# Expert rows of the sparse tokens begin when half of tile 1's heads are picked, in a two-block transformer kernel on one core

## What is computed

```python
def peer_ffn(h, w_q, sub_k1, sub_k2, expert_u, expert_v):
    q = (ht @ w_q).reshape(T, PEER_HEADS, PEER_QDIM)
    s1 = jnp.einsum('thd,nd->thn', q[..., :PEER_HALF], sub_k1).astype(jnp.float32)
    s2 = jnp.einsum('thd,nd->thn', q[..., PEER_HALF:], sub_k2).astype(jnp.float32)
    v1, i1 = lax.top_k(s1, PEER_TOPK)
    v2, i2 = lax.top_k(s2, PEER_TOPK)
    cand = (v1[..., :, None] + v2[..., None, :]).reshape(T, PEER_HEADS, PEER_TOPK * PEER_TOPK)
    ...
    vals, pos = lax.top_k(cand, PEER_TOPK)
    experts = jnp.take_along_axis(cand_idx, pos, axis=-1)
    gates = jax.nn.softmax(vals, axis=-1)
    ...
        u = expert_u[ec]
        a = jnp.einsum('cd,chkd->chk', xc, u).astype(jnp.float32)
        w = (jax.nn.gelu(a) * gc).astype(xc.dtype)
        return jnp.einsum('chk,chkd->cd', w, expert_v[ec])
```

## Time and profile before

| | |
|---|---|
| median of 3 runs | 1836.27 us (1835.15 to 1836.65) |
| the profiled execution: its time | 1835.7 us |
| its span, first to last instruction | 1833.9 us |
| PE busy | 1767.6 us (96%) |
| DVE busy | 1032.5 us (56%) |
| data moved | 439.57 MB, mean 240 GB/s |
| mean granted TensorE clock | 0.984 |

### The profile page before, as it was taken

One profiled execution on the slowest core, in us unless ns is written; L12 is line 12 of the kernel. 1 busy time (PEld: TensorE's weight loads), 2 busy tenths in 40 slices (PEclk: granted clock), 3 DMA queues, 4 the chain that ended last, 5 costly groups with the idle time before them and its releaser, 6 DMA issues.

```text
span 1833.9 us, 28803 instructions
## 1 busy us (share of the span) xinstructions
PE 1767.6 (96%) x11513; PEld 1477.1 (81%) x11513; DVE 1032.5 (56%) x2254; ACT 254.9 (14%) x603; POOL 295.1 (16%) x280
## 2 busy tenths in 40 slices
PE   8999989999999999999999689999999999999996
PEld 6478647886999999999999566789965977699942
DVE  1421342386964988899443653259984213269964
ACT  1013540120444111000000010111100001111100
POOL 0200000003333454344332510000000000000000
PEclk9999999999999999999999789999999999999998
DMA  7435232437999999999999963274454434354551
GB/s 277 162 124 175 72 113 92 166 117 286 418 416 416 414 416 411 369 415 414 416 416 418 368 259 115 92 252 162 165 180 159 162 138 148 128 184 161 171 174 46
DMA packets 76397, 439.57 MB, mean 240 GB/s; under 512 B 8530, under 2 KB 8560, under 8 KB 37504
## 3 DMA queue, kind: packets, MB, share of 16 engines
q1 hardware_dynamic: 42336, 304.11, 44.2%
q0 software_dynamic: 32528, 126.44, 17.5%
q10 hardware_dynamic: 1424, 7.47, 1.0%
HBM read 432.67 MB, written 5.24 MB: 239 GB/s over the span
## 4 chain that ended last, share of the span: by engine, by line
PE 70%; DMA 13%; DVE 9%; issue 6%; ACT 1%; POOL 0%; DVEq 0%; POOLq 0%
PE ps L1067 12%; PE ps L484 10%; PE ps L526 8%; PE ps L827 7%; PE ps L835 7%; PE ps L442 6%; DMA arena<-v_rows,sparse_pairs 6%; DMA arena<-u_rows,sparse_pairs 6%; PE ps L1088 4%; PE ps L451 4%; DVE arena L1850 2%; DVE arena L1749 2%; PE ps L695 2%; PE ps L742 2%; PE ps L848 1%
## 5 line engine op out<-in xcount | busy, mean ns | idle before, releaser
L827 PE MATMUL ps<-xT,ring 128*128 128x152 f32 x2048 | 271.6, 294 | 3.5 <-DVE sel L1859 3.4
L827 PEld LDWEIGHTS ps<-xT,ring 128*128 128x128 f32 x2048 | 267.2, 191 | 4.4 <-DVE sel L1859 3.7
L835 PE MATMUL ps<-arena,ring 128*128 128x152 f32 (+1 forms) x2048 | 269.6, 293 | 0.1
L835 PEld LDWEIGHTS ps<-arena,ring 128*128 128x128 f32 x2048 | 265.5, 190 | 0.8 <-issue 0.8
L484 PE MATMUL ps<-ring,arena 128*128 128x512 f32 x416 | 181.4, 592 | 0.4 <-ACT arena L1371 0.4
L1850 DVE SCALAR_TENSOR_TENSOR arena<-arena,sparse_dots 128x1024 f32<-128x1024 f32 x105 | 134.7, 1283 | 76.1 <-DMA arena<-v_rows,sparse_pairs 68.4
L526 PEld LDWEIGHTS ps<-xT,ring 128*128 128x128 f32 x1536 | 173.4, 192 | 3.0 <-issue 2.9
L526 PE MATMUL ps<-xT,ring 128*128 128x128 f32 x1536 | 174.1, 275 | 0.0
L1749 DVE CUSTOM_DVE_ANT_0 arena<-arena 128x1024 f32<-128x1024 f32 x107 | 128.2, 1223 | 78.6 <-DMA arena<-u_rows,sparse_pairs 71.3
L2271 POOL DMA_INDIRECT arena<-u_rows,sparse_pairs x107 | 129.7, 1213 | 188.9 <-DVE sparse_dots L1749 153.5
L2271 POOL DMA_INDIRECT arena<-v_rows,sparse_pairs x107 | 130.2, 1216 | 179.8 <-DVE arena L1850 121.6
(11 more groups left out here) (305 smaller groups left out, 2108.0 us busy)
## 6 DMA issues: line engine op xcount, KB each, us to landing
ring<-stream SPq DMA_DIRECT2D x288, 1024.0 KB
arena<-second_params POOLq DMA_DIRECT2D x6, 1024.0 KB, 5.2
arena<-kv_scratch POOLq DMA_DIRECT2D x2, 2048.0 KB, 13.3
kv_scratch<-arena POOLq DMA_DIRECT2D x2, 1024.0 KB, 6.7
kv_scratch<-arena ACTq DMA_DIRECT2D x2, 1024.0 KB
arena<-held_params ACTq DMA_DIRECT2D x1, 2048.0 KB
arena<-u_rows,sparse_pairs POOLq DMA_INDIRECT x107
arena<-v_rows,sparse_pairs POOLq DMA_INDIRECT x107
```

The lines of the kernel that those rows point to most:

```text
L827: ins = pe.matmul(ps[:, o % 2, 0:DENSE], w[:, (o % 2) * D + k * P:(o % 2) * D + (k + 1) * P], xT[:, k, 0:DENSE], start=(k == 0), stop=(k = ...
L835: ins = pe.matmul(ps[:, 4 + k // 2, c:c + DENSE], w[:, (o % 2) * D + k * P:(o % 2) * D + (k + 1) * P], H[:, n, :], start=False, stop=last, ...
```

## The change

Three things, all on the way of the rows. (1) The expert numbers of the first four heads of tile 1 are staged and sent as soon as they are picked (`stage_rows(0)`, `rows_of(0)`), those of the last four after the second pick. To make each half cover all 128 partitions, the 64 pairs are dealt alternately: even ones to one half of the partitions, odd ones to the other. The gates, which are known later, go by a DMA of their own, issued behind u row 16. (2) Two row dots stand behind each of tile 1's last four heads, and the targets rise by the 8 dots: `DOTS_ROUTING` 30 to 38, `DOTS_FIRST` 50 to 56. (3) `LAST_ADDS` falls from 21 to 16. `U_FIRST` and `ROWS` stay.

```diff
+PH_LATE = 4
+DOTS_HEAD = 2
+DOTS_EARLY = DOTS_HEAD * PH_LATE
-DOTS_ROUTING = 30
-DOTS_FIRST = 50
-LAST_ADDS = 21
+DOTS_ROUTING = 38
+DOTS_FIRST = 56
+LAST_ADDS = 16
...
+            def stage_rows(half):
+
+                link(dve.memset(mark_cell[:], 0.0))
+                rows, c = slice(P - SPARSE_A, P), slice(half * PAIRS_HALF // 2, (half + 1) * PAIRS_HALF // 2)
+                first, second = (routed[rows, 1, n, half * PAIRS_HALF:(half + 1) * PAIRS_HALF]
+                                 .rearrange("p (m r) -> p r m", r=2) for n in range(2))
+                for r, dst in enumerate((pairs, pairs_out)):
+                    ins = dve.scalar_tensor_tensor(dst[rows, 0, c].bitcast(U32), first[:, r], float(P), second[:, r],
+                                                   ALU.mult, ALU.add)
+                ins.then_inc(pairs_staged, 1)
+                if half == 0:
+                    dve.wait_ge(x_sparse_ready, 1)
...
                 if h == PH - 1:
                     shift_gates()
+                if h >= PH - PH_LATE:
+                    row_dots(DOTS_HEAD)
                 if h % 4 == 3:
                     pick(1, h - 3, 4)
+                    stage_rows(h // 4)
...
+            def rows_of(half):
+
+                c = slice(half * PAIRS_HALF // 2, (half + 1) * PAIRS_HALF // 2)
+                pool.wait_ge(pairs_staged, half + 1)
+                pool.dma_start(pairs[0:SPARSE_A, 0, c], pairs_out[SPARSE_A:P, 0, c]).then_inc(pairs_in, 16)
+
+            rows_of(0)
             pool.wait_ge(pairs_in, 16)
...
                 fetch_u(m)
-                if m == 3:
+                if m == ROWS + DOTS_EARLY - 1:
+                    rows_of(1)
+                    pool.wait_ge(pairs_in, 32)
+                if m == ROWS + DOTS_EARLY + 1:
+                    pool.wait_ge(pairs_staged, 3)
+                    pool.dma_start(pairs[0:SPARSE_A, 1, 0:PAIRS_HALF], pairs_out[SPARSE_A:P, 1]).then_inc(pairs_in, 16)
                     for e in range(SETS_B):
```

More of the change, by code:

```diff
@@ L1328, in _ @@
             act.wait_ge(sel_ready, 2)
-            act.wait_ge(pairs_in, 16 * (1 + SETS_B))
+            act.wait_ge(pairs_in, 16 * (3 + SETS_B))
             with act.Fori(HALF_BLOCKS // 2, EXPERT_BLOCKS // 2) as n:
@@ L1800, in _ @@
                     shift_gates()
+                if h >= PH - PH_LATE:
+                    row_dots(DOTS_HEAD)
                 if h % 4 == 3:
                     pick(1, h - 3, 4)
-            dve.wait_ge(x_sparse_ready, 1)
+                    stage_rows(h // 4)
             for turn_no, i in enumerate(TILES):
@@ L1820, in _ @@
                     up_rows, b_rows = slice(P - SPARSE_A, P), slice(0, P // 2)
[L1821 to L1828, removed]
+                    gates_of = gf[up_rows].rearrange("p (m r) -> p r m", r=2)
+                    for r, dst in enumerate((pairs, pairs_out)):
+                        dve.tensor_copy(dst[up_rows, 1, 0:PAIRS_HALF], gates_of[:, r])
+                    dve.scalar_tensor_tensor(pairs_out_b[b_rows, 0, 0:P].bitcast(U32), routed[b_rows, 1, 0, :],
+                                             float(P), routed[b_rows, 1, 1, :], ALU.mult, ALU.add)
+                    dve.tensor_copy(pairs_out_b[b_rows, 1, 0:P], gf[b_rows]).then_inc(pairs_staged, 1)
                     dve.wait_ge(pairs_staged, 3)
@@ L1896, in _ @@
                 if hf:
-                    dve.wait_ge(pairs_in, 16 * (1 + SETS_B))
+                    dve.wait_ge(pairs_in, 16 * (3 + SETS_B))
                     weigh(slice(0, PAIRS_HALF), dot_gelu, weight_ready)
@@ L2263, in _ @@
             row_inverse(1)
-            pool.wait_ge(pairs_staged, 3)
-            pool.dma_start(pairs[0:SPARSE_A, :, 0:PAIRS_HALF], pairs_out[SPARSE_A:P]).then_inc(pairs_in, 16)
+            def rows_of(half):
[3 more added lines that the diff above has]
+            rows_of(0)
             pool.wait_ge(pairs_in, 16)
@@ L2287, in _ @@
                 if m == PAIRS_HALF:
-                    pool.wait_ge(pairs_in, 16 * (1 + SETS_B))
+                    pool.wait_ge(pairs_in, 16 * (3 + SETS_B))
                 fetch_u(m)
-                if m == 3:
+                if m == ROWS + DOTS_EARLY - 1:
[4 more added lines that the diff above has]
+                    pool.dma_start(pairs[0:SPARSE_A, 1, 0:PAIRS_HALF], pairs_out[SPARSE_A:P, 1]).then_inc(pairs_in, 16)
                     for e in range(SETS_B):
```

## The result

The changed kernel takes 1826.55 us (median of 4 runs, 1824.81 to 1829.2) against 1836.46 us (4 runs): ratio 0.9948, 95% interval 0.9933 to 0.9962, so 9.9 us faster. Predicted were 1832.0 us, with a range from 1827.0.

The account below looks back on a forecast made before the run. PE, busy for 96% of the span, was taken as the bound. Terms 0 + 0 + 0 + 1.0 - 5.3 = -4.3 us took the profiled 1835.7 to 1831.4, plus 0.6 for the median: 1832.0 us, range 1827.0 to 1837.5.

Parts of the forecast that it names:

- The pairs, POOL and row 0: Tile 1's routing: pairs sent at about 391.7, row 0 issued at about 395.3, dot 0 at 404.6.
- the step that failed: Row 0, from issue to dot: 9.3 us, bounds 8 and 10.5, instead of the earlier 10.5.
- The term for `sel`: PE's 3.4 us wait for `sel` stays, its copy at 594.40: 0 us, bounds -1.5 and +2.
- the prediction's own exchange: Row issues beside the weights in the u phase: 31 in 100 us, 3.2 us a row.
- the first rival: PE's wait for `sel` goes, some 3 us won: 1829.0, at most 1827; chance 0.12.
- The lead and the barrier: Start of the v side: the lead is absorbed there and does not get through, 0 us.
- The gates' own DMA: POOL behind row 16: some 2 us more while it waits for dots anyhow, 0 us.
- The moved adds: Layer's end: fold starts 1.0 us later, second wait gone, full clock gives 5.3 us back; -4.3 us.
- The clock was given back: Fold and `ab_pool(1)` at full clock, 5.3 us back; the rival that it is not: 1837.3, chance 0.14.
- The slower rival: DVE's stall before tile 0's routing grows, break-even 10.3 us late; 1839.0 at 13 us late; chance 0.09.

Follow-up runs that it names:

- The experiment that moved the store: Kernel before, with ACT's 1 MB store of k1 moved from beside row 0 to behind the copies of v1: 1842.54 us, ratio 1.0032.
- The kernel with lateness put back: Changed kernel plus two idle DVE operations (some 4.5 us together) behind the first two early dots: 1831.06 us, ratio 0.9971 to the kernel before.

## Why the prediction was wrong

**The pairs, POOL and row 0.** The pairs' DMA came at 393.12, or 391.5 without the late start (forecast 391.7). From there to row 0's issue it took 4.5 us, 0.9 more than forecast. Then came **the step that failed**: "at a DMA share of 0.31 I take 9.3 us, with 8 and 10.5 as bounds". It measured 4.9, and 4.7 to 4.9 in the six other profiles in which row 0 is fetched early and used at once. I took a time measured beside other transfers and gave back only a little for an emptier stretch. The share ahead of the fetch does not tell the two apart: in the kernel before it was 0.33 from 427 to 431 us, as low as the 0.31 that I used. It rose to 0.79 from 431 to 436 and to 1.01 from 436 to 441, while row 0 was under way; in the changed kernel it was 0.60 from 397.6 to 402.5, with the row's own bytes in it. The experiment that moved the store shows 3.7 us of the 10.5 to be that one transfer's; the step from 6.8 to 4.9 was not tested apart. The first dot came at 402.51, or 400.9 without the late start (forecast 404.6).

**The term for `sel`, "0 us, bounds -1.5 and +2".** It rests on "DVE is 6 us late and 8 dots ahead". DVE was 1.1 us late. Of these 5 us, 3.7 are row 0's. About 1 lies behind the shift of the gates, where the forecast had 17 us up to the next dot (from 430 to 447) and 15.88 were measured: in the kernel before, DVE waited 3.02 us there for ACT's exponential as well, and that wait is gone too. By the prediction's own exchange, a row for 3.2 us, those 5 us are 1.5 rows more than the six that `DOTS_FIRST` gives away, and `sel` came 4.0 us earlier after the start of the u side; PE's first matmuls with one-hots start at 596.90 instead of 598.87, which is 3.6 us earlier against the same start. Putting the lateness back by hand cost 4.5 us. This is the first rival, which had 0.12; its price of 3 us was about right (3.6 in the traces; 4.1 us between the kernel with the moved adds alone and the changed one, 3.7 between the changed kernel with 21 last adds and the kernel before, and 2.9 for one dot fewer without early rows). The wait is not the same in every execution: of the five profiles with early dots, `DOTS_FIRST` at 56 and nothing that makes DVE late, one showed 3.4 us of it, one 1.5 and three none. The three without it are the three with the late start. Whether that is chance, and what moves `sel` by 4 us when DVE is on time, is open.

**The lead and the barrier, "Term: 0 us": right.** 14.12 us of idle time against 14.11. The kernels with `U_FIRST` 100 and 104 show that it is the barrier that holds the lead back: four rows before it bring 5.4 us and eight 10 us, where without early rows four bring 3.0 and eight 2.3.

**The gates' own DMA, 0 us.** No wait in the list of PE points to it; it was not run alone.

**The moved adds, "-4.3": right in its mechanism, too small.** The kernel with lateness put back is the one that the prediction describes, and its one-hots start 0.2 us behind those of before (599.07 and 598.87), so that the end can be compared there term by term. To be read against the earlier trace rows:

```profile
1042.60 8.98 PE L925 MATMUL ps<-xT,ring 128*128 128x128 f32 x64 [24.04 <-DVE xT L1935]
...
1065.52 3.76 PE L957 MATMUL ps<-small,arena 128*128 128x64 f32 x32 [0.20 <-DVE arena L1869]
1069.12 7.39 PE L925 MATMUL ps<-xT,ring 128*128 128x128 f32 x64
1076.35 7.03 PE L936 MATMUL ps<-ring,xT 128*128 128x512 f32 x16
```

- the fold starts at 1065.52 instead of 1065.88. Forecast was 1.0 later, it is 0.4 earlier (0.6 counted from the one-hots). PE was to reach it at 1066.86 with a first restart as slow as before; the 64 matmuls behind the first wait took 8.98 us instead of 10.20. The prediction had this as a bound and not in the sum. In the changed kernel itself they took 10.12 us, so this piece is not constant. PE was so early here that it waited 0.20 us for the last add again; the fold still took 3.60 us.
- the fold: 3.60 us from its start to the next group instead of 6.85, 3.25 given back (3.4 forecast)
- `ab_pool(1)`: 7.23 instead of 8.81, 1.6 (1.9 forecast)

Together 0.4 + 3.25 + 1.6 = 5.2 us. The moved adds alone, without early rows, gave 6.3 us in medians. Over the whole program the span is 6.3 us shorter. The 1.1 us between stand behind the last computing instruction, where the rows show only the transfer of the output (2.0 us from issue to landing) and then nothing. The last lines of the timeline of DVE, in the kernel before and in the changed one:

```profile
1821.51 0.69 DVE L2022 TENSOR_TENSOR xres<-xres,arena 128x512 f32<-128x512 f32 x1
```

```profile
1814.94 0.69 DVE L2038 TENSOR_TENSOR xres<-xres,arena 128x512 f32<-128x512 f32 x1
```

From there to the end of the span are 11.7 us before (1833.9 - 1822.2) and 10.7 us after (1826.3 - 1815.6). All profiled kernels built from the one before have the longer end and those from the changed one the shorter (between the two in the kernel without early dots). Its cause is open. It explains a further 1 us of the miss.

**The sum.** Between the two profiled executions 1.6 us are lost ahead of the change, 3.6 won at `sel`, 4.6 at the end of the layer (1081.54 - 1074.96 = 6.58 at the matmuls behind `ab_pool(1)`, less the 1.97 at the one-hots) and 1.0 behind the last instruction: 7.6 us, the difference of the spans. The medians differ by 9.9, since the profiled execution of after was 1.5 us over its median and that of before 0.8 under. Forecast was 4.3. Of the 5.6 us that were missing, 3.6 are the wait for `sel` and 1.0 stand behind the last instruction; the last 1 us fits what the end of the layer gave above the forecast in the kernel with lateness put back (5.2), but lies within the spread of the executions.

The range reached down to 1827.0 for the case that the first rival comes alone. It came together with a larger gain at the end, and so the result lies below the range.

**The other rivals.** The clock was given back in all kernels with 16 last adds; with 21 the fold took 7.05 us in each. The slower rival asks for a DVE that is 10.3 us late. It was not near: DVE was 1.1 us late, and with 4.6 us more the time was still under that of the kernel before.

## What to carry to other kernels

- The latency of a transfer belongs to the traffic it was measured in. When a change moves it to an empty stretch, do not take a small discount on the crowded value: ask which transfers run while this one is under way, in both places, and let the lower bound be what is left without them.
- A lead has a value only if it is spent ahead of the next barrier. Ask what it could carry past it: here eight rows, for twice the gain of the change, by one constant and the order of POOL's waits that follows from it.
- Where one engine waits twice for another that is busy throughout, put the two waits together: the wait costs the same, and the clock has one restart less.

## What the runs showed that I had not expected

- One fetched row of 0.5 MB took 10.5 us from issue to use beside a store and the weights, 6.8 us without the store, and 4.9 us at the place where the other transfers had left the DMA share at 0.31 before the change.
- 4.61 us more of DVE at 404 us cost 4.5 us in the median of the whole program, although 190 us lie between them and PE's wait for `sel`. From 470 to 590 us the DMA share was 1.02 in this kernel and in the changed one, so there was no room in which the delay could be made up.
- Kernels that are the same up to `sel` copied it 128.5 to 134.1 us after the start of the u side. One pair of traces says little about a gain of 4 us there.
- The end of the program behind the last computing instruction differs by 1.0 us between kernels that are the same there.
